# An order of loads, sums and half projections changed in a two-block transformer kernel on one core

## The reference

```python
# first block: a gated mixer, then sliding-window attention (16 query heads of 64, 2 key heads)
h = x + gmlp_mixer(rms_norm(x, a_norm_g), ...)        # ends in y @ a_w_out  (2048 x 1024)
kv = rms_norm(h, kv_norm_g) @ w_kv + b_kv             # k rotated; k, v shared by all heads
q, g = split(rms_norm(h, b_norm_g) @ w_in)            # q + b_q, rotated
h = h + (softmax_with_sink(q k / 8, window=128) @ v * silu(g)) @ w_out
x = rms_norm(h, final_norm_g)
# second block
mod = silu(c) @ ada_w + ada_b                          # 6 x 1024: sh1, sc1, g1, sh2, sc2, g2
h = rmsnorm(x, norm1_g) * (1 + sc1) + sh1
proj = h @ w_in                                        # q, k, v of 8 + 8 heads
o_na  = attention over a 2-D neighbourhood, with a bias table
o_dil = attention over three dilated windows
y = concat(rmsnorm(o_na, g_na), rmsnorm(o_dil, g_dil)) @ w_out
x = x + g1 * y
h = rmsnorm(x, norm2_g) * (1 + sc2) + sh2
# then: 8 x 256 queries, scores against 2 x 128 keys, top 16, experts up, gelu, experts down, a norm
```

## Time and profile before

| | before |
|---|---|
| median of three executions | 1352.52 us |
| profiled execution | 1354.3 us |
| its span, first to last instruction | 1352.5 us |
| mean granted TensorE clock | 0.982 |
| TensorE, its weight loads | 1293.9, 1169.2 us busy |
| VectorE, ScalarE, GpSimd | 995.4, 758.8, 387.9 us busy |
| moved | 249.15 MB, 184 GB/s |

### The profile page before, as it was taken

One profiled execution on the slowest core, in us unless ns is written; L12 is line 12 of the kernel. 1 busy time (PEld: TensorE's weight loads), 2 busy tenths in 40 slices (PEclk: granted clock), 3 DMA queues, 4 the chain that ended last, 5 costly groups with the idle time before them and its releaser, 6 DMA issues.

```text
span 1352.5 us, 26489 instructions
## 1 busy us (share of the span) xinstructions
PE 1293.9 (96%) x8560; PEld 1169.2 (86%) x8560; DVE 995.4 (74%) x1848; ACT 758.8 (56%) x1285; POOL 387.9 (29%) x257
## 2 busy tenths in 40 slices
PE   7999997999998789999999999999999999999996
PEld 7999997888998789999999977777888888888885
DVE  6999988897885777896889855555666666666666
ACT  6444444556755465557888744444555555555554
POOL 1199812215141037788777500000000000000000
PEclk9999998999998799999999999999999999999998
DMA  9978775453655245554333355555755565565561
GB/s 361 330 250 260 252 240 196 156 159 114 233 201 173 77 156 173 171 172 154 121 115 110 112 184 172 185 172 170 250 188 188 189 191 188 188 187 188 186 193 66
DMA packets 68317, 249.15 MB, mean 184 GB/s; under 512 B 7968, under 2 KB 8352, under 8 KB 67488
## 3 DMA queue, kind: packets, MB, share of 16 engines
q1 hardware_dynamic: 59040, 214.14, 47.6%
q10 hardware_dynamic: 9216, 34.21, 7.4%
HBM read 245.70 MB, written 2.62 MB: 184 GB/s over the span
## 4 chain that ended last, share of the span: by engine, by line
PE 69%; DVE 3%; POOL 2%; ACT 2%; issue 1%; ACTq 0%; DVEq 0%; POOLq 0%
PE ps L2281 26%; PE ps L1782 17%; PE ps L2292 10%; PE ps L2294 5%; PE ps L2252 4%; PE ps L2047 1%; PE ps L2155 1%; PE ps L1939 1%; ACT pr L586 1%; POOL x L1729 1%; POOL tmp L1722 1%; PE ps L1958 1%; ACT WH L470 1%; PE ps L1928 1%; PE ps L2193 1%
## 5 line engine op out<-in xcount | busy, mean ns | idle before, releaser
L932 DVE TENSOR_TENSOR WL<-raw,WH 128x1024 fp32r<-128x1024 f32 x322 | 411.8, 1282 | 160.9 <-ACT WH L470 156.6
L470 ACT ACTIVATE WH<-raw 128x1024 fp32r<-128x1024 f32 x394 | 414.6, 1055 | 170.3 <-PE ps L2281 88.7
L1782 PE MATMUL ps<-X,WH 128*128 128x256 f32 x1888 | 353.8, 288 | 0.3 <-issue 0.2
L1782 PEld LDWEIGHTS ps<-X,WH 128*128 128x128 f32 x1888 | 297.5, 194 | 1.1 <-issue 0.7
L1782 PE MATMUL ps<-X,WL 128*128 128x256 f32 x944 | 269.4, 285 | 0.0
L2292 PE MATMUL ps<-X,WH 128*128 128x512 f32 x576 | 205.4, 397 | 0.0
L2281 PE MATMUL ps<-WH,wvH 128*128 128x512 f32 x500 | 202.1, 404 | 1.4 <-DVE wvL L1537 1.4
L2281 PE MATMUL ps<-WH,wvL 128*128 128x512 f32 x500 | 197.1, 394 | 0.0
L2281 PE MATMUL ps<-WL,wvH 128*128 128x512 f32 x500 | 196.7, 393 | 0.0
L1747 POOL TENSOR_TENSOR WL<-raw,WH 128x1024 fp32r<-128x1024 f32 x72 | 173.6, 2415 | 74.9 <-ACT WH L470 74.8
L1782 PEld LDWEIGHTS ps<-X,WL 128*128 128x128 f32 x944 | 182.8, 194 | 0.0
(11 more groups left out here) (311 smaller groups left out, 2300.7 us busy)
## 6 DMA issues: line engine op xcount, KB each, us to landing
raw<-stream SPq DMA_DIRECT2D x394, 512.0 KB, 3.4
ada<-adaT ACTq DMA_DIRECT2D x48, 512.0 KB, 3.5
bias<-att_bias ACTq DMA_DIRECT2D x9, 512.0 KB, 4.7
x<-xT SPq DMA_DIRECT2D x2, 512.0 KB, 5.5
ws<-wsT SPq DMA_DIRECT2D x1, 1024.0 KB, 11.3
lng<-rows SPq DMA_DIRECT2D x1, 1024.0 KB, 7.0
lnb<-rows SPq DMA_DIRECT2D x1, 1024.0 KB, 7.9
bsb<-rows SPq DMA_DIRECT2D x1, 1024.0 KB, 8.8
```

Source lines behind the costliest of these rows:

```text
L470: act.activation(WH[:, slot, :], raw[:, slot, :], ACT.Copy).then_inc(h_done, 1)
L932: dve.tensor_tensor(WL[:, slot, :], raw[:, slot, :], WH[:, slot, :].bitcast(F32), ALU.subtract).then_inc(l_done, 1)
L1782: mm = pe.matmul(out_ap, a(kc), b(kc), start=(first and kc == 0 and i == 0), stop=(last and kc == KC - 1 and i == 2))
```

## The change

In the first output projection the ada load stands behind both roundings and one round earlier sums end (`n < KC - 2`); the swa steps take ada tiles 30 to 37 in place of 31 to 39, and tiles 38 and 39 stand between the low parts of the value tiles. GpSimd's `rope` is split in `rope_cos` and `rope_sum`, with the second product ahead of the first sum. In swa steps 2 to 7 TensorE does `turn_out` ahead of `turn_probs`. In mixed step 1 reciprocal and refinement of the final norm stand together, right behind `soft_in`; in step 7 the low part of chunk `C_COUT + 3` takes the place of the ada sum, and `ada_tile(47)` follows in the projection. `steps` is the same edit on ScalarE, VectorE and TensorE: mixed steps end at 7 (TensorE at 9), and the last pair of heads is written out. The root of the neighbourhood half's norm moves into step 7; the last exponentials stand behind it, the last turn and copies go by half. The first four projection tiles, in banks given by `cout_bank`, are done head block by head block (`cout_part`). The second half's norm and the second norm are made per token on two columns: two matmuls of one column per token tile sum the squares, the root, reciprocal and refinement are on 128x2, two diagonals carry the result, and one matmul spreads it (`token_sums`, `token_root`, `token_spread`). In these sums TensorE takes the last squares itself, so GpSimd's loops of `add_square(28)` and `(32)` lose one round (`Fori(0, 4)` to `(0, 3)`, `(0, KC)` to `(0, KC - 1)`). The branches for steps 8 and 9 of `mix_step`, `cout_half`, `rms(5)`, `rms(6)` and their loops are gone. In `early_down` each weight's rounding and low part stand a round later, so behind the next value's. Cut to its core, eight spaces of indent taken off:

```diff
@@ -419,6 +420,10 @@
+def cout_bank(n):
+    return (0, 1, 4, 5, 2, 3, 0, 1)[n]
@@ -557,16 +562,19 @@
         hi(C_AOUT + 3 + 2 * n, g)
-        load_ada(25 + n, g)
         hi(C_AOUT + 4 + 2 * n, g)
...
+        if n < KC - 2:
+            load_ada(25 + n, g)
@@ -612,7 +620,7 @@
         if m < 8:
-            load_ada(33 + m, g)
+            load_ada(31 + m, g)
@@ -620,14 +628,14 @@
-    def steps(eng, step):
+    def steps(eng, step, last=11):
...
-        with eng.Fori(1, 3) as g:
+        with eng.Fori(1, 2) as g:
             step(2, g)
             step(3, g)
-        for m in range(8, 11):
+        for m in range(6, last):
             step(m)
@@ -668,6 +676,7 @@
     hi(C_V2 + 3)
+    load_ada(39)
     for n in range(2):
@@ -690,6 +699,7 @@
         v_token(n, 4 + n)
+    load_ada(40)
@@ -706,34 +716,50 @@
-        if m == 8:
-            hi(C_COUT + 3)
         if g is not None or m >= 3:
             sq_tile(24 + m - 3, oT, ot_done, m - 2, m - 3, g, 2)
-        if 1 <= m <= 8:
+        if m >= 1:
             exps(8 + m - 1, g, False)
...
-        if m == 8:
+        if m == 7:
+            hi(C_COUT + 3)
+        if g is not None or m < 7:
+            load_ada(41 + m, g)
+        if m >= 1:
+            pt_out(8 + m - 1, g, 4)
+            if g is not None or m < 7:
+                load_bias(m + 1, g)
+        if m == 7:
             root(4)
...
+    steps(act, mix_step, 8)
+    def norm_high(n):
+        act.wait_ge(yf_ready, AG + 8 + n + 1)
+        act.activation(YH[:, 1 + n, :], FY[:, n, :], ACT.Copy).then_inc(yh_ready, 1)
+    exps(15, None, False)
+    for h, turned in enumerate(((pt_first, 1), (pt_mm, 16))):
+        act.wait_ge(*turned)
+        if h == 0:
+            act.wait_ge(o_mm, 15)
+        act.activation(pT[:, h, 0:4, :].rearrange("p k t -> p (k t)"), ps[:, 6 + h, 0:4 * P],
+                       ACT.Copy).then_inc(pt_ready, 1)
+    sq_tile(29, oT, ot_done, 6, 5, None, 1)
     norm_high(0)
-    root(5)
+    sq_tile(30, oT, ot_done, 7, 6, None, 1)
     norm_high(1)
+    act.wait_ge(ot_done, NPAIR)
+    act.activation(tmp[3][:, :], oT[:, 7, :], ACT.Square).then_inc(sq_ready, 1)
+    for n in range(2, 4):
+        norm_high(n)
+    act.wait_ge(m_ready, 6)
+    act.activation(st1, st0, ACT.Sqrt).then_inc(root_ready, 1)
+    for n in range(4, 8):
+        norm_high(n)
@@ -852,10 +879,11 @@
-        hi(C_V1 + 3 + j, g)
+        if g is not None or j >= 1:
+            hi(C_V1 + 2 + j, g)
...
+    hi(C_UV + 2)
@@ -1079,7 +1107,7 @@
-        if n < KC - 1:
+        if n < KC - 2:
             ada_tile(24 + n, g)
@@ -1229,10 +1257,8 @@
-        if m == 0:
-            ada_tile(31)
         if m < 8:
-            ada_tile(32 + m, g)
+            ada_tile(30 + m, g)
@@ -1316,66 +1342,91 @@
     modulated(0, s1, mod[:, 0:8], R[:, 0, :], between_tiles)
-    for n in range(8, 11):
-        lo(C_V2 + n)
+    lo(C_V2 + 8)
+    ada_tile(38)
+    lo(C_V2 + 9)
+    lo(C_V2 + 10)
+    ada_tile(39)
...
-                                 in1=R[:, n // 4, :], op0=ALU.mult, op1=ALU.mult).then_inc(yf_ready, 1)
+                                 in1=R[:, 0, :] if n < 4 else ps[:, 7, T:2 * T], op0=ALU.mult,
+                                 op1=ALU.mult).then_inc(yf_ready, 1)
...
+    def mix_out(m, g=None):
...
+    def token_root(m, r):
+        dve.wait_ge(root_ready, m)
+        link(dve.reciprocal(rstd, st1))
+        newton(rstd, st0, st1, r_ready)
+        dve.wait_ge(r_ready, m)
+        for t in range(NT):
+            dve.tensor_scalar(R[:, r, t * P:(t + 1) * P], ident, rstd[:, t:t + 1], None,
+                              ALU.mult).then_inc(rd_ready, 1)
     def mix_step(m, g=None):
...
+        lo(C_QK + 2 * m + 3, g)
         if g is not None or m >= 3:
...
+            mix_out(m, g)
+        if m >= 1:
             soft_in(8 + m - 1, g, False)
...
         if m == 1:
...
-        if g is None and m == 2:
             newton(R[:, 1, :], first_mean, nt[:, :], r_ready)
...
+        if m >= 2:
+            o_out(8 + m - 2, g)
+        lo(C_QK + 2 * m + 4, g)
+        if m == 7:
+            dve.wait_ge(psn_ready, 5)
+            dve.tensor_scalar(nm[:, :], ps[:, 0, T:2 * T], 2.0 / D, EPS_B, ALU.mult, ALU.add).then_inc(m_ready, 1)
...
+            soft_sum(8 + m - 1, g, False)
+        if m == 7:
+            lo(C_COUT + 3)
+        else:
+            ada_tile(40 + m, g)
+    steps(dve, mix_step, 8)
+    soft_in(15, None, False)
+    mix_out(8)
+    o_out(14, None)
+    dve.wait_ge(root_ready, 5)
+    link(dve.reciprocal(R[:, 0, :], nt[:, :]))
+    newton(R[:, 0, :], nm[:, :], nt[:, :], r_ready)
+    dve.wait_ge(r_ready, 5)
+    soft_sum(15, None, False)
+    normed(0)
+    o_out(15, None)
+    normed_low(0)
+    mix_out(9)
+    normed(1)
+    mix_out(10)
+    normed_low(1)
+    for n in range(2, 4):
+        normed(n)
         normed_low(n)
+    ada_tile(47)
+    dve.wait_ge(psn_ready, 6)
+    dve.tensor_scalar(st0, ps[:, 7, 0:NT], 2.0 / D, EPS_B, ALU.mult, ALU.add).then_inc(m_ready, 1)
+    token_root(6, 1)
+    dve.wait_ge(psn_ready, 7)
...
-    rms(5, D // 2, EPS_B, ps[:, 7, 0:T])
...
     for n in range(4, 8):
@@ -1386,25 +1437,25 @@
+    for n in range(4, KC):
+        cout_step(n)
+    dve.wait_ge(psn_ready, 8)
+    dve.tensor_scalar(st0, ps[:, 7, 0:NT], 1.0 / D, EPS_B, ALU.mult, ALU.add).then_inc(m_ready, 1)
+    token_root(7, 0)
+    dve.wait_ge(psn_ready, 9)
+    modulated(1, s2, mod[:, 24:32], ps[:, 7, T:2 * T])
@@ -1536,10 +1587,11 @@
-        lo(C_V1 + 3 + j, g)
+        if g is not None or j >= 1:
+            lo(C_V1 + 2 + j, g)
...
+    lo(C_UV + 2)
@@ -1691,22 +1743,29 @@
-    rope(0, ks[:, 0, :], None)
-    for m in range(2):
-        rope(m + 1, qs[:, m, :], None)
+    rope_cos(0)
+    rope_cos(1)
+    rope_sum(0, ks[:, 0, :], None)
+    rope_sum(1, qs[:, 0, :], None)
+    rope_cos(2)
+    rope_sum(2, qs[:, 1, :], None)
@@ -2004,28 +2063,30 @@
+        if 2 <= m < 8:
+            turn_out(m - 2, g)
...
-        if m >= 2:
-            turn_out(m - 2, g)
+        if m >= 8:
+            turn_out(m - 2, None)
...
+    steps(pe, swa_step, 10)
@@ -2133,48 +2194,83 @@
-        if 1 <= m <= 8:
+        if 1 <= m < 8:
...
+        if m == 8:
+            pe.wait_ge(pt_ready, 30)
+            for h, turned in enumerate((pt_first, pt_mm)):
+                pe.wait_ge(p_ready, 62 + 2 * h)
+                for k in range(4):
+                    mm = pe.transpose(ps[:, 6 + h, k * P:(k + 1) * P], pr_h[:, h, k * P:(k + 1) * P], ident)
+                mm.then_inc(turned, 1)
...
-    steps(pe, mix_step)
-    spread(5, sacc_done, 32, qb[:, 0, :])
...
+    steps(pe, mix_step, 10)
+    def cout_part(n, k0, k1):
...
+        if k0 == 0:
+            pe.wait_ge(l_done, C_COUT + n + 1)
+        for kc in range(k0, k1):
+            pe.wait_ge(yl_ready, AG + 8 + kc + 1)
+            for i, (a, b) in enumerate(((wh, YH), (wh, YL), (wl, YH))):
+                mm = pe.matmul(ps[:, cout_bank(n), 0:T], a(kc), b[:, 1 + kc, :],
+                               start=(kc == 0 and i == 0), stop=(kc == KC - 1 and i == 2))
+        if k1 == KC:
+            mm.then_inc(chunk_done, 1)
+    def token_sums(square, squares, acc, adds):
+        pe.wait_ge(sq_ready, squares)
+        pe.wait_ge(sacc_done, adds)
+        for t in range(NT):
+            ts = slice(t * P, (t + 1) * P)
+            mm = pe.matmul(ps[:, 7, t:t + 1], square[:, ts], ones[:, 0:1], start=True, stop=False)
+            if t == NT - 1:
+                mm.then_inc(sacc_done, 1)
+            mm = pe.matmul(ps[:, 7, t:t + 1], acc[:, ts], ones[:, 0:1], start=False, stop=True)
+        mm.then_inc(psn_ready, 1)
+    def token_spread(count, r):
+        pe.wait_ge(rd_ready, count)
+        pe.matmul(ps[:, 7, T:2 * T], ones[:, :], R[:, r, :], start=True, stop=True).then_inc(psn_ready, 1)
     pe.wait_ge(m_ready, 5)
+    pe.wait_ge(s_ready, 16)
+    for kc in range(4):
+        for n in range(4):
+            cout_part(n, kc, kc + 1)
+        if kc == 1:
+            token_sums(tmp[3], 33, qb[:, 0, :], 31)
+    token_spread(NT, 1)
+    for kc in range(4, 6):
+        for n in range(4):
+            cout_part(n, kc, kc + 1)
...
-        if n == 2:
+        cout_part(n, 6, 8)
+    for n in range(4, KC):
+        if n < 6:
             pe.wait_ge(ot_done, NPAIR)
...
+        else:
+            pe.wait_ge(x_ready, 24 + n - 5)
+        feature_tile(C_COUT + n, None, cout_bank(n), YH, YL, 1)
...
-    spread(6, sacc_done, 40, tmp[5][:, :])
+    token_sums(tmp[4], 41, tmp[5], 39)
...
     for i in range(4):
+        if i == 2:
+            token_spread(2 * NT, 0)
         t = i // 2
```

## The result

The changed kernel takes 1322.84 us in the median of four runs (1321.41 to 1324.66), against 1354.22 of the kernel before in the runs beside it: a ratio of 0.977, with a 95% interval of 0.9746 to 0.9794.

The account below looks back on a forecast made before the run. TensorE was taken as the bound, busy 1293.9 of 1352.5 us, leaving only 58.6 us idle and low-clock losses to win. Seven terms summed to -22.6 us, from 1352.5 to 1329.9, range 1324 to 1339.

Parts of the forecast that it names:

- Term 7: Early down tiles: a value's rounding no longer stands behind a weight's, removing TensorE's last listed wait; -1.4 us.
- Term 1: First output projection to first queries: moved ada load and sum, hidden table load bring tanh earlier; -7.7 us.
- Term 2: Swa steps: the output's two transposes fill TensorE's wait for the exponentials; -0.5 us, bounds 0 to 0.9.
- Term 3: Before the mixed steps: ada sums 38 and 39 burden VectorE ahead of the first key copy; +0.5 us.
- Term 4: Mixed steps: GpSimd's rescale of x ends earlier, removing a wait and the low clock behind it; -7.8 us.
- Term 5: End of mixed attention and projection: earlier last softmax, less new waits around the token norm; -4.0 us, bounds 0 to 6.
- Term 6: Second norm to query projection: shorter norm chain and perhaps half the low clock behind it; -1.7 us.
- rival B: End of mixed attention and projection: table loads, VectorE's wait and token norm take back the gain; 1333.9 us, chance 0.20.
- D: Projection through query tiles: TensorE stays at clock 0.50, making the kernel slower; 1383.5 us, chance 0.03.
- the row: Last exponentials: traced table load of 1.28 us without the skill's extra drain, which would start them 2.8 later (1332.7 total).

Follow-up runs that it names:

- the loops: Kernel before with only the step loops of ScalarE, VectorE and TensorE cut from two rounds to one, steps 6 and 7 written out: 1351.22 us (0.9983).
- `aout_full`: Kernel before with the first output projection's ada loads behind both roundings and the ada sums moved as in the change: 1346.19 us (0.9946).
- `end_alone`: Kernel before with only the change's mixed attention end, projection by heads, both token norms and one-round step loops: 1347.68 us (0.9952).

## Why the prediction was wrong, and where it was right

**Term 7 is the step that failed.** "-1.4, the last wait of the earlier trace rows" took the listed wait for the whole price; it was 9.9 in the trace and 10.2, 10.5 and 10.1 in the times of three kernels. The mechanism was named half: the chain ran through VectorE's low part of the weight, which stood ahead of the value's, and not through ScalarE's order of the two roundings. It was also the one term without bounds. What would have shown it was there before: the weight loads' waits, the first matmul of each tile 0.50 long, and the sum of the chain, 1.06 + 1.23 + 0.42 = 2.71 without the gaps between, nearly a tile's 2.79. "After it TensorE never waits" read a busy engine as one that ran at its pace. The text had named the sign of this itself, that the time from 506 us to the end changes by more than 2; the lead grows by more than 9 from there on.

With 9.9 in place of 1.4 the sum is -31.1, and 31.4 were measured. That this comes so close is luck in part: terms 5 and 6 were 2.6 too high, and an edit without a term, the loops, brought 2.3 in time and 3.6 in the trace. The parts tried alone do add up: 7.8 (`aout_full`) + 7.4 + 6.3 (with the loops) + 10.2 = 31.7.

**Term 1** (-7.7): 8.7 in the trace, 7.8 in time by `aout_full`. The load's place gave 3.6, more than the 2.5 to 3 of the text; sums and table load gave the rest. GpSimd's order gave nothing. The wait for the third rotary input was to stay near 3 and fell to 1.6.

**Term 2** (-0.5): the turns are worth nothing that can be told. The 2.0 us that the window steps lost all lie behind the first values (55.0 and 53.0), and the loops alone give 1.8 of them. In the sum the loops, an edit that the text left without a term, filled what terms 5 and 6 lacked.

**Term 3** (+0.5): 0; by the traces' own time (0.6 less than by the table) the lead is 10.2 ahead of the two sums (value tiles at 337.34 and 327.16) and 10.2 behind them (mixed step 1 at 369.18 and 358.96).

**Term 4** (-7.8): 7.4 in time, 7.7 in the trace.

**Terms 5 and 6** (-4.0 and -1.7): 3.1 together by `end_alone` less the loops in the trace. Term 5 was 1.1 there (up to the diagonals) and 1.8 in the changed kernel, whose lead by own time grows from 18.7 at the values before the last to 20.5. Up to the projection's start things went as the text has them for low clock: it starts at 458.1 in the time frame of the text, for 457.8. The text then took 4.0, between its 3.0 for low clock and 5.6 for full, and the clock was low. The rest went in the projection, which gave 3.9 back: one wait of 1.5 for the low parts, 0.8 of TensorE's own time for the sums, the spread, a wait of 0.4 for a weight ahead of tile 4, and 22 matmuls at low clock where it had 17 before. Term 6 was 0.9 up to the first query matmul and 1.1 behind it by the clock, 2.0 for 1.7. So rival B (term 5 is 0) came nearer to term 5 than the forecast did; all that speaks against it is the 1.1 to 1.8 that is left. D did not occur: the clock was low for 5 us after the projection starts.

**The table load.** ScalarE in the changed kernel, from the sqrt's table load to the exponentials:

```profile
427.74 1.28 ACT L479 ACT_TABLE_LOAD   x1
429.04 0.42 ACT L479 ACTIVATE nt<-nm 128x256 f32<-128x256 f32 x1
429.47 1.28 ACT L594 ACT_TABLE_LOAD   x1
430.76 0.51 ACT L594 ACTIVATE pr<-s,small 128x256 f32<-128x256 f32 x1
```

The exponentials start 0.01 behind the second load. The drain of 1.38 us that the Trainium skill ("ScalarE: Activation LUTs", section "What ACT_TABLE_LOAD costs") adds to each switch does not show, behind either load or ahead of it; the row was right.

What stays open: whether the register and branch instructions are what a loop of two rounds costs, and what makes the low stretch in the window steps come or stay away. A version without token norms was not tried, so their price rests on the trace.

## What to carry to other kernels

A busy TensorE isn't at its pace: compare a group's mean duration between its first and its other matmuls, read the weight loads' waits beside the matmuls', and where several engines feed each tile, add up the chain from the slot's release to the next start and set it against the tile's time. A stall of 0.16 us in 52 tiles (8.2 us) outweighs the longest wait outside the start-up (4.6). Before two traces are compared, see whether both have the same stretches of low clock: one of 3.4 us was worth 1.5 here, and it came in two of five profiles of the same instructions. And price every edit of a diff, loop bounds too.

## What was not expected of the hardware

In a wait of 2.2 us on TensorE (429.8 to 432.0) the granted clock fell to half at 430.7 and stayed there for 13.7 us; 16 matmuls whose result nothing reads, put into that wait, brought the following work back to full clock and 2.5 us net. A wait as long before the first values of the window attention was followed by 3.4 us of low clock in two of five profiles, and by none in three. A loop over three engines cut from two rounds to one took 0.3 to 0.5 us less a step, in the steps written out (9.4 against 9.7 to 9.9) and in its own round (19.6 against 20.5 for two steps).
